# A two-layer decoder trunk on one core: both attention heads of a step together, the imaginary S5 drive from a row-swapped copy of u, and the next step's small loads spread over the step

## The chip, the cores and the metric

The kernel runs on one core of one Trainium2 chip. The metric is the device time of one execution in microseconds. All arithmetic is float32, with the large products in a split form of it. PE is the matrix engine, DVE the vector engine, ACT the scalar engine, POOL the general one, and SP the queue from which most DMAs are issued.

## What is computed

Two layers over x (512 positions x 2048 channels). Each layer scales and shifts x by values from a conditioning vector, projects it to twelve groups of 512 channels, runs four branches on them, and projects their gated outputs back, with a residual and a layer norm.

```python
h = x * (1.0 + scale[:, None]) + shift[:, None]
proj = h @ w_in[l]
y_a = a_b * causal_dwconv(a_c * a_x, conv_a[l]) * jax.nn.silu(a_g)
y_b = dilated_attention(q, k, v, rel_bias).reshape(Bsz, S, BR) * jax.nn.silu(b_g)
y_c = rglru_branch(c_x, conv_c[l], conv_c_b[l], ...) * jax.nn.silu(c_g)
y_d = s5_branch(d_u, ...) * jax.nn.silu(d_g)
y = jnp.concatenate([y_a, y_b, y_c, y_d], axis=-1) @ w_out[l]
x = layer_norm(ALPHA * x + (1.0 + gate[:, None]) * y, ln_g[l], ln_b[l])
```

Attention has 8 heads of 64 channels; its three dilation patterns are merged into one causal softmax with an additive bias per head. The S5 branch drives a complex diagonal state of 64 per group of 16 channels: a real and an imaginary drive (`bu_re`, `bu_im`), a scan, and an output product.

## The kernel before

After a prologue (conditioning sums, bias tables, the transposed and scaled x in `op_hi` and `op_lo`), each layer runs a **branch loop** of four steps (`CT`), and then the output projection (L917 to L945). A step handles 128 channels of every one of the twelve groups, so two attention heads (h = 0, 1) and four S5 tiles (q = 0 to 3).

**PE** walks a step in 24 halves (`HALF`), n = 0 to 23: two for each of the twelve units in `UNITS`. A half is 24 matmuls of 128x512: sixteen with the high part of the weights (L886, L887) and eight with the low part (L893). After half n PE does the small parts that `put(n, ...)` placed there (L856 to L874): `s5_drive` (two matmuls of 32 rows, real into bank 2 and imaginary into bank 3, L785), `s5_output` (L791, L792), `lru_gates` (L801), `scores` (64 rows, L811), `p_turn` (transposes of the probabilities, L820), `weigh` (probabilities times v, 64 columns, L828), `v_turn` and `ada_sum` (L846). These small float32 matmuls stand in the trace as two passes each. Score banks are 5 and 6. Before the change, tiles t of one head alternate between them, and the second head waits until the first has left the banks.

**The weights**: SP loads a half's slice into `raw` (L387), ACT writes `w_hi` (L553) and the negated slice `w_lo` (L556), and POOL issues a DMA that adds `raw` to `w_lo` (L505). PE waits for that DMA before L893.

**SP** issues in program order. Between the slices stand the pieces of `w_ada` for the conditioning of the next part (`ada_load`, L379), which wait until DVE has consumed an earlier piece: two per place in layer 0, one in layer 1. After the last half come the ten small loads of the next step (`step_loads`, L353): S5 and LRU parameters and two bias tiles.

**DVE** runs one list per step (L1001 to L1166), every dependent operation waiting for the one before: parameters of the step, the convolution, per S5 tile `s5_tile` (six operations in, the scan with its carries, six out), the LRU, `score_max` (scores plus bias with a running maximum, L1087; it frees the score bank), `normalise` (L1095), and the gates. `ada(2, 1)` consumes two pieces in layer 0 and one in layer 1. **ACT** does the exponentials of a head (`exps`, L591), copies of transposed probabilities (`p_copy`, L599) and evictions of units, between the weight splits.

```python
for q, (at_drive, at_output) in enumerate(((5, 9), (7, 12), (10, 16), (13, 19))):
...
for h, at in ((0, 10), (1, 17)):
    for t in range(ST):
        put(at + t // 2, scores, h, t)
```

## Time and profile before

| | |
|---|---|
| median of 3 runs | 1981.57 us (1981.14 to 1985.36) |
| profiled execution, its own time | 1983.35 us |
| its span, first to last instruction | 1981.6 us |
| PE busy (matmul) | 1793.6 us, 91% |
| DVE / ACT / POOL busy | 1251.7 / 767.1 / 232.9 us |
| mean granted clock of PE | 0.947 of full speed |
| share of PE in the chain that ended last | 65% (DVE 25%, DMA 4%) |

Times in the trace are microseconds from the start of the span. A row of a timeline gives start, busy time, engine, line, operation, output and input, shape, count, and in brackets the idle time before it and what ended that. Busy times of matmuls overlap: the start of the next row tells when PE was done with issuing the group.

### The profile page before, as it was taken

How to read it: one execution, taken by the hardware profiler on the slowest of the kernel's cores; microseconds unless marked ns; L12 is line 12 of the kernel's file. 1: busy time of each engine (PE TensorE's matmuls, PEld its weight loads, DVE VectorE, ACT ScalarE, POOL GpSimd, SP SyncE). 2: the span in 40 equal slices, each digit the busy share in tenths (PEclk: the TensorE clock that was granted, in tenths of full speed). 3: DMA queues.
4: the chain of work that ended last, by engine and by line, in shares of the span. 5: the costliest groups of instructions: out<-in, count | busy, mean ns of one | idle time of the engine just before them, and what ended most of it. 6: DMA issues, size and time to landing. Idle time of an engine off the chain costs nothing.

```text
span 1981.6 us, 22817 instructions
## 1 busy us (share of the span) xinstructions
PE 1793.6 (91%) x7335; PEld 1323.1 (67%) x7335; DVE 1251.7 (63%) x2361; ACT 767.1 (39%) x1014; POOL 232.9 (12%) x281
## 2 busy tenths in 40 slices
PE   2359999999999999989996999999999999979993
PEld 1347677667667766658885767766876776748882
DVE  5976863883586488456663585486478368543656
ACT  2235344344444443431116544444444454441110
POOL 2331111111111111100004111111111111100000
PEclk9569999999899999999997999999999999989997
DMA  7999679678777986737656867866976886727322
GB/s 274 375 308 236 168 197 216 175 190 208 179 192 194 219 209 161 201 113 258 191 170 177 198 162 181 204 165 168 210 181 154 198 193 167 171 64 255 132 91 85
DMA packets 322945, 376.07 MB, mean 190 GB/s; under 512 B 27064, under 2 KB 224032, under 8 KB 319784
## 3 DMA queue, kind: packets, MB, share of 16 engines
q1 hardware_dynamic: 294632, 272.36, 42.8%
q0 software_dynamic: 28224, 102.77, 28.2%
q8 instruction: 26, 0.43, 0.1%
q14 instruction: 63, 0.52, 0.1%
HBM read 261.81 MB, written 10.51 MB: 137 GB/s over the span
## 4 chain that ended last, share of the span: by engine, by line
PE 65%; DVE 25%; DMA 4%; issue 4%; ACT 1%; SPq 1%; DVEq 0%; POOL 0%; ACTq 0%; POOLq 0%
PE bank L886 12%; PE bank L893 12%; PE bank L887 12%; DVE work L1185 8%; PE bank L931 6%; PE bank L930 6%; PE bank L942 6%; DVE work L1193 3%; DVE ada_acc L1193 3%; PE bank L828 2%; PE bank L811 2%; PE bank L785 2%; PE bank L905 2%; DVE work L1061 2%; DVE work L1062 2%
## 5 line engine op out<-in xcount | busy, mean ns | idle before, releaser
L886 PE MATMUL bank<-op_hi,w_hi 128*128 128x512 f32 x1536 | 625.2, 407 | 0.0
L887 PE MATMUL bank<-op_lo,w_hi 128*128 128x512 f32 x1536 | 607.9, 396 | 0.0
L553 ACT ACTIVATE w_hi<-raw 128x1024 fp32r<-128x1024 f32 x196 | 207.7, 1060 | 525.2 <-PE bank L887 470.9
L893 PE MATMUL bank<-op_hi,w_lo 128*128 128x512 f32 x1536 | 382.6, 391 | 12.0 <-DMA w_lo<-raw 12.0
L886 PEld LDWEIGHTS bank<-op_hi,w_hi 128*128 128x128 f32 x1536 | 293.8, 191 | 113.7 <-issue 54.5
L893 PEld LDWEIGHTS bank<-op_hi,w_lo 128*128 128x128 f32 x1536 | 288.8, 189 | 75.3 <-DMA w_lo<-raw 15.5
L887 PEld LDWEIGHTS bank<-op_lo,w_hi 128*128 128x128 f32 x1536 | 293.8, 191 | 60.8 <-issue 1.9
L505 POOL DMA_DIRECT2D w_lo<-raw x196 | 170.5, 870 | 1198.1 <-ACT w_lo L556 1175.5
L1193 DVE SCALAR_TENSOR_TENSOR ada_acc<-ada_in,cond,ada_acc 128x512 f32<-128x512 f32 (+1 forms) x234 | 181.5, 776 | 132.9 <-DMA ada_in<-in_w_ada 117.5
L556 ACT ACTIVATE w_lo<-raw 128x1024 fp32r<-128x1024 f32 x196 | 207.0, 1056 | 127.4 <-PE bank L893 127.3
L930 PE MATMUL bank<-w_hi,op_hi 128*128 128x512 f32 x512 | 200.0, 391 | 0.0
L931 PE MATMUL bank<-w_hi,op_lo 128*128 128x512 f32 x512 | 199.2, 389 | 0.0
L702 ACT ACTIVATE w_hi<-raw 128x1024 fp32r<-128x1024 f32 x60 | 63.7, 1062 | 248.2 <-PE bank L931 242.4
L1185 DVE TENSOR_TENSOR w_lo<-raw,w_hi 128x1024 fp32r<-128x1024 f32 x60 | 73.5, 1225 | 118.7 <-PE bank L942 115.5
L1185 DVE TENSOR_TENSOR work<-bank,rot 128x512 f32<-128x512 f32 x128 | 88.4, 690 | 65.1 <-PE bank L785 61.5
L942 PE MATMUL bank<-w_lo,op_hi 128*128 128x512 f32 x512 | 126.4, 389 | 0.0
L1185 DVE TENSOR_TENSOR work<-work 128x512 f32<-128x512 f32 (+2 forms) x170 | 112.6, 662 | 5.8
L930 PEld LDWEIGHTS bank<-w_hi,op_hi 128*128 128x128 f32 x512 | 96.1, 188 | 20.4 <-issue 0.5
L931 PEld LDWEIGHTS bank<-w_hi,op_lo 128*128 128x128 f32 x512 | 96.1, 188 | 20.4 <-issue 0.5
L942 PEld LDWEIGHTS bank<-w_lo,op_hi 128*128 128x128 f32 x512 | 96.1, 188 | 19.9
L1185 DVE TENSOR_TENSOR work<-work,rot 128x512 f32<-128x512 f32 x128 | 88.4, 690 | 3.3
L514 POOL TENSOR_TENSOR op_lo<-work,op_hi 128x512 fp32r<-128x512 f32 x32 | 51.5, 1618 | 308.2 <-ACT work L570 307.6
(203 smaller groups left out, 1625.8 us busy)
## 6 DMA issues: line engine op xcount, KB each, us to landing
w_lo<-raw POOLq DMA_DIRECT2D x196, 512.0 KB, 4.7
raw<-in_w_in SPq DMA_DIRECT2D x192, 512.0 KB, 4.0
ada_in<-in_w_ada SPq DMA_DIRECT2D x256, 256.0 KB, 4.4
raw<-in_w_out SPq DMA_DIRECT2D x64, 512.0 KB, 4.1
raw<-in_w_ada SPq DMA_DIRECT2D x27, 512.0 KB, 7.0
ada_in<-in_w_ada SPq DMA_DIRECT2D x18, 512.0 KB, 7.1
rot<-in_w_ada SPq DMA_DIRECT2D x10, 512.0 KB, 6.6
bias_t<-in_w_ada SPq DMA_DIRECT2D x9, 512.0 KB, 7.1
```

The source lines that it names most:

```text
L505: pool.dma_start(w_lo[:, n % NHL, :], raw[:, n % NRAW, :], accum_op=ALU.add)\
L553: act.activation(w_hi[:, n % NHL, :], raw[:, n % NRAW, :], ACT.Copy).then_inc(s.hi_done.sem, 1)
L556: act.activation(w_lo[:, n % NHL, :], raw[:, n % NRAW, :], ACT.Copy, scale=-1.0)\
L702: act.activation(w_hi[:, n % NHL, :], raw[:, n % NRAW, :], ACT.Copy).then_inc(s.hi_done.sem, 1)
L886: pe.matmul(o, w_hi[:, n % NHL, w], op_hi[:, k, :], start=k == 0, stop=False)
L887: mm = pe.matmul(o, w_hi[:, n % NHL, w], op_lo[:, k, :], start=False, stop=False)
L893: mm = pe.matmul(o, w_lo[:, n % NHL, w], op_hi[:, k, :], start=False, stop=k == KT - 1)
L930: pe.matmul(o, op_hi[:, k, x_], w_hi[:, n % NHL, w_], start=k == 0, stop=False)
L931: mm = pe.matmul(o, op_lo[:, k, x_], w_hi[:, n % NHL, w_], start=False, stop=False)
L942: mm = pe.matmul(o, op_hi[:, k, x_], w_lo[:, n % NHL, w_], start=False, stop=k == KT - 1)
L1185: return dve.tensor_tensor(o, a, b, op)
L1193: return dve.scalar_tensor_tensor(o, a, sc, b, op0, op1)
```

## The change

Six things change in the branch loop:

- The scores of both heads are computed together: tile t of head 0 goes to bank 5 and of head 1 to bank 6, each in two column pieces that alternate between the heads. They stand behind halves 9, 10, 12 and 13.
- `p_turn` and `weigh` take both heads in three groups of key blocks (`TURNS`), behind halves 16, 18, 20 and 18, 20, 22. The matmuls of `weigh` alternate between the heads, whose outputs are columns 0 to 63 and 64 to 127.
- Exponentials are head by head after halves 15 and 16 on ACT, both waiting for the one maximum signal. Probabilities of head 1 lie in other buffers (`prob_of`).
- The imaginary drive reads `u_swap`, a copy of u with its two 64-row halves exchanged, so that its rows are 64 away from those of the real drive. ACT makes the copy in two operations of 64 rows, and DVE writes the imaginary coefficients in two operations more per step.
- `s5_tile` is split into `s5_in`, `s5_scan` and `s5_out`, and DVE's list is reordered around `score_max`.
- The loads of the next step are split: LRU behind slice 12, bias behind slice 18, S5 at the end.

```diff
+u_swap = work[:, 17, :]
-p_t = work[:, 14:16, :]
+p_t = [(work[:, 14, :], work[:, 15, :]), (q_t, k_t)]
+prob_of = [[prob[:, at:at + P * (t + 1)] for t, at in enumerate(P_AT)],
+           [ada_acc[:, 2, 0:P], prob[:, 1280:1536], ada_acc[:, 2, P:S], v_t]]
+
+TURNS = ((0,), (1, 3), (2,))
+TURN_AT = {0: 0, 1: 0, 3: 3 * P, 2: 0}
...
-        def step_loads(step):
+        def s5_loads(step):
...
+        def lru_loads(step):
+
+            if step:
+                sp.wait_ge(s.full[6].sem, s.full[6].at(1, step - 1))
...
+        def bias_loads(step):
+
+            if step:
+                sp.wait_ge(s.to_act.sem, s.to_act.at(2, step - 1))
...
+                if step < CT - 1:
+                    if n == 12:
+                        lru_loads(step + 1)
+                    if n == 18:
+                        bias_loads(step + 1)
...
             if step < CT - 1:
-                step_loads(step + 1)
+                s5_loads(step + 1)
...
+            def p_copy(g):
+                n = sum(P * (ST - kb) for kb in TURNS[g])
+                if g != 1:
+                    act.wait_ge(s.pv_done.sem, s.pv_done.at(g, ct))
+                for h in range(2):
+                    act.wait_ge(s.full[5 + h].sem, s.full[5 + h].at(1 + ST + g + 1, ct))
+                    act.activation(p_t[h][g % 2][:, 0:n], bank[5 + h][:, 0:n], ACT.Copy).then_inc(s.p_copy.sem, 1)
...
-                    copy("d_u", u_d)
+                    ps, free = unit("d_u")
+                    act.wait_ge(s.gate_used[1].sem, s.gate_used[1].at(0, ct))
+                    act.activation(u_d, ps, ACT.Copy)
+                    for h in range(2):
+                        swapped = act.activation(u_swap[64 * h:64 * h + 64, :], ps[64 - 64 * h:128 - 64 * h, :], ACT.Copy)
+                    swapped.then_inc(free.sem, 1)
...
                 if n == 13:
-                    exps(0)
                     gate("c_g", 0, 0)
...
+                if n in (15, 16):
+                    exps(n - 15)
                 if n == 15:
+                    act.wait_ge(s.full[3].sem, s.full[3].at(SQ, ct))
                     gate("d_g", 1, 0)
-                if n == 16:
-                    p_copy(0, 0)
-                    p_copy(0, 1)
+                if n in (18, 20, 22):
+                    p_copy((n - 18) // 2)
...
-                    fill(2 + i, pe.matmul(bank[2 + i][:, :], s5_w[32 * q:32 * q + 32, i, :],
-                                          u_d[32 * q:32 * q + 32, :], start=True, stop=True))
+                for i, u in enumerate((u_d, u_swap)):
+                    row = 32 * ((q + 2 * i) % SQ)
+                    fill(2 + i, pe.matmul(bank[2 + i][:, :], s5_w[row:row + 32, i, :], u[row:row + 32, :],
+                                          start=True, stop=True))
...
+                n = P * (t + 1)
+                for h in range(2):
+                    is_free(5 + h, 1 + t)
+                for w in (slice(0, n // 2), slice(n // 2, n)):
+                    for h in range(2):
+                        heads = slice(64 * h, 64 * h + 64)
+                        mm = pe.matmul(bank[5 + h][:, w], q_t[heads, P * t:P * (t + 1)], k_t[heads, w],
+                                       start=True, stop=True)
...
+                for kb in TURNS[g]:
+                    n = P * (ST - kb)
+                    for w in (slice(0, n // 2), slice(n // 2, n)) if kb % 2 else (slice(0, n),):
+                        for h in range(2):
+                            mm = pe.matmul(bank[7][64 * h:64 * h + 64, P * kb + w.start:P * kb + w.stop],
...
+            for t, at in enumerate((9, 10, 12, 13)):
+                put(at, scores, t)
             put(11, v_turn)
-            for h, at in ((0, 14), (1, 21)):
...
+            for g, (at_turn, at_weigh) in enumerate(((16, 18), (18, 20), (20, 22))):
+                put(at_weigh, weigh, g)
+                put(at_turn, p_turn, g)
...
-        s5_tile(1, 2, 1)
-        score_max(0, (0, 1))
-        ada(2, 1)
-        score_max(0, (2, 3))
-        ada(2, 1)
+        score_max(0)
+        s5_in(1)
+        s5_scan(1)
+        ada(2, 1)
+        score_max(1)
+        s5_out(1)
+        ada(2, 1)
+        score_max(2)
+        s5_in(2)
+        ada(2, 1)
+        score_max(3)
+        s5_scan(2)
+        ada(2, 1)
+        s5_out(2)
         normalise(0)
-        s5_tile(2, 2, 1)
+        ada(2, 1)
+        normalise(1)
         own(silu2(0, "c_g", gx[:, 0, :]), s.own)
...
-        s5_tile(3, 2, 1)
-        score_max(1, (0, 1))
-        ada(2, 1)
-        score_max(1, (2, 3))
+        s5_in(3)
+        s5_scan(3)
+        ada(2, 1)
+        s5_out(3)
```

**PE behind half 10** (`raw` slice 10, `work` holds u, q, k, their copies and the probabilities). Before, the drive of tile 2 and the first two score tiles of head 0:

```order
L785 MATMUL bank<-work,s_w 128x512 [waits free2_0]
L785 MATMUL bank<-work,s_w 128x512 [waits free3_0]
L811 MATMUL bank<-work 128x128 [waits free5_0,free1_0,free0_0]
L763 REGISTER_ALU
L811 MATMUL bank<-work 128x256 [waits free6_0]
```

Now, at the same place:

```order
L807 MATMUL bank<-work,s_w 128x512 [waits free3_0,free2_0]
L807 MATMUL bank<-work,s_w 128x512
L783 REGISTER_ALU [waits free5_0]
L835 MATMUL bank<-work 128x128 [waits free6_0]
L835 MATMUL bank<-work 128x128 x3
```

The two drives now wait for both banks at once, and one score tile (t = 1) of both heads stands in four pieces of 128 columns where two tiles of one head stood.

**PE, first `weigh` and the transposes behind it.** Before, behind half 15:

```order
L828 MATMUL bank<-work 64x512 [waits free7_0,p_copy_0]
L825 REGISTER_ALU
L828 MATMUL bank<-work 64x384 [waits p_copy_0]
L820 MATMUL bank<-ident,work 128x128 [waits p_copy_0,p_norm_0]
L820 MATMUL bank<-ident,work 128x128
```

Now, behind half 18:

```order
L861 MATMUL bank<-work 64x512 [waits free7_0,p_copy_0]
L861 MATMUL bank<-work 64x512
L849 MATMUL bank<-ident,work 128x128 [waits p_copy_0]
L849 MATMUL bank<-ident,work 128x128 x3
L849 MATMUL bank<-ident,work 128x128 [waits p_copy_0]
```

Key block 0 of both heads stands side by side, three halves later, and blocks 1 and 3 are turned behind it.

**SP at the end of a step.** Before:

```order
L380 DMA ada_in<-in_w_ada 128x512 [waits ada_used_0] x2
L363 DMA work<-in_s_b_re 128x4x16 [waits to_act_0,c_done_0]
L363 DMA work<-in_s_b_im 128x4x16
L367 DMA work<-in_s_c_re 128x64
L367 DMA work<-in_s_c_im 128x64
L372 DMA lru_w<-in_lru_wa 64x64 x2
L372 DMA lru_w<-in_lru_wx 64x64 x2
L375 DMA bias_t<-bias_tile_scratch 128x512 x2
L387 DMA raw<-in_w_in 128x8x128 [waits raw_used_0] x2
```

Now, behind slice 12 of the step, and at its end:

```order
L399 DMA raw<-in_w_in 128x8x128 [waits raw_used_0]
L379 DMA lru_w<-in_lru_wa 64x64 [waits full6_0]
L379 DMA lru_w<-in_lru_wa 64x64
L379 DMA lru_w<-in_lru_wx 64x64 x2
L399 DMA raw<-in_w_in 128x8x128 [waits raw_used_0]
```

```order
L365 DMA work<-in_s_b_re 128x4x16 [waits c_done_0]
L365 DMA work<-in_s_b_im 128x4x16
L369 DMA work<-in_s_c_re 128x64
L369 DMA work<-in_s_c_im 128x64
L399 DMA raw<-in_w_in 128x8x128 [waits raw_used_0] x2
```

Four of the ten loads remain between the last slice of a step and the first of the next.

## Rows read from the trace of the kernel before

**Rows 1.** Busy time of two of the eight steps of the branch loop, core 0, microseconds

```profile
309.00:485.50 176.50, 171.02 (x690) 123.05 (x690) 116.53 (x246) 75.02 (x100) 20.85 (x24) 0.97 0.79 194
...
1412.60:1578.20 165.60, 164.61 (x681) 119.69 (x681) 104.40 (x229) 76.72 (x101) 20.83 (x25) 1.00 0.77 182
```

**Rows 2.** Timeline of PE, layer 1, third step: start, busy, line

```profile
1438.43 1.98 PE L893 MATMUL bank<-op_hi,w_lo 128*128 128x512 f32 x8
...
1443.88 1.97 PE L893 MATMUL bank<-op_hi,w_lo 128*128 128x512 f32 x8
...
1445.78 1.98 PE L785 MATMUL bank<-work,s_w 32*128 32x512 f32 x4
...
1451.45 1.97 PE L893 MATMUL bank<-op_hi,w_lo 128*128 128x512 f32 x8
...
1458.65 1.97 PE L893 MATMUL bank<-op_hi,w_lo 128*128 128x512 f32 x8
```

**Rows 3.** The same timeline: `weigh` (L828), then `scores` (L811) of one head

```profile
1519.75 1.72 PE L828 MATMUL bank<-work 128*64 128x512 f32 x4
...
1521.40 0.55 PE L820 MATMUL bank<-ident,work 128*128 128x128 f32 x3
...
1529.19 0.86 PE L828 MATMUL bank<-work 128*64 128x256 f32 x4
...
1535.65 0.92 PE L811 MATMUL bank<-work 64*128 64x128 f32 x4
...
1542.17 1.77 PE L811 MATMUL bank<-work 64*128 64x384 f32 x4
```

**Rows 4.** The same timeline: the eight passes of `ada_sum`

```profile
1577.12 1.05 PE L846 MATMUL bank<-ones,ada_acc 128*128 128x1 f32 x8
```

**Rows 5.** Waits of PE over the whole span: total, times, longest

```profile
PE bank L811 <- DVE soft L1087: 12.9, 8, 3.9
```

**Rows 6.** Timeline of PE, layer 0, after halves 10 and 12 of two steps

```profile
385.23 1.97 PE L893 MATMUL bank<-op_hi,w_lo 128*128 128x512 f32 x8
...
402.88 1.98 PE L893 MATMUL bank<-op_hi,w_lo 128*128 128x512 f32 x8
...
731.46 1.98 PE L893 MATMUL bank<-op_hi,w_lo 128*128 128x512 f32 x8
...
754.85 1.98 PE L893 MATMUL bank<-op_hi,w_lo 128*128 128x512 f32 x8
```

**Rows 7.** Timelines of PE and of SP, layer 0, around step boundaries

```profile
344.96 2.55 PE L893 MATMUL bank<-op_hi,w_lo 128*128 128x512 f32 x8 [3.16 <-DMA w_lo<-raw]
...
347.44 3.78 PE L785 MATMUL bank<-work,s_w 32*128 32x512 f32 x4
...
466.73 2.16 SPq L372 DMA_DIRECT2D lru_w<-in_lru_wx  x2
...
502.06 1.13 SPq L380 DMA_DIRECT2D ada_in<-in_w_ada  x2
```

**Rows 8.** Timeline of DVE, layer 1, third step

```profile
1492.96 0.69 DVE L1087 CUSTOM_DVE_ANT_0 work<-bank,bias_t 128x512 f32<-128x512 f32 x1
...
1496.45 1.66 DVE L1189 TENSOR_SCALAR work<-work,soft 128x128 f32<-128x128 f32 x4
...
1498.14 1.42 DVE L1185 TENSOR_TENSOR work<-bank,rot 128x512 f32<-128x512 f32 x2
...
1502.49 0.42 DVE L1061 TENSOR_TENSOR_SCAN work<-s_k,work 128x128 f32<-128x128 f32 x1
...
1509.30 0.75 DVE L1193 SCALAR_TENSOR_TENSOR ada_acc<-ada_in,cond,ada_acc 128x512 f32<-128x512 f32 x1
...
1509.97 1.41 DVE L1185 TENSOR_TENSOR work<-work,rot 128x512 f32<-128x512 f32 x2
```

**Rows 9.** End of a step on DVE, and the wait of PE behind a layer's loop

```profile
1582.28 0.43 DVE L1189 TENSOR_SCALAR y_t<-work 128x512 f32 x1 [0.16 <-DVE work L1193]
...
846.79 13.80 PE L905 MATMUL bank<-y_t,work 128*128 128x512 f32 x26 [9.36 <-DMA work<-in_s_w_glu]
```

More of the change, by code:

```diff
@@ L61 @@
 ADA_PLACES = 16
-OWN_STEPS = (168, 167)
+OWN_STEPS = (170, 169)
 ROWS = {}
@@ L814, in p_turn @@
-                    def p_turn(h, kb):
-                        b = 5 + kb % 2
-                        pe.wait_ge(s.p_norm.sem, s.p_norm.at(h + 1, ct))
-                        if kb >= 2:
-                            pe.wait_ge(s.p_copy.sem, s.p_copy.at(ST * h + kb - 1, ct))
-                        for t in range(kb, ST):
-                            mm = pe.transpose(bank[b][:, P * (t - kb):P * (t - kb + 1)],
-                                              prob[:, P_AT[t] + P * kb:P_AT[t] + P * (kb + 1)], ident[:, :])
-                        fill(b, mm)
@@ L824, in weigh @@
-                    def weigh(h, kb):
-                        pe.wait_ge(s.p_copy.sem, s.p_copy.at(4 * h + kb + 1, ct))
-                        if h == 0 and kb == 0:
-                            is_free(7, 1)
-                        pe.matmul(bank[7][64 * h:64 * h + 64, P * kb:S], v_s[:, kb, 64 * h:64 * h + 64],
-                                  p_t[:, kb % 2, 0:P * (ST - kb)], start=kb == 0, stop=kb == ST - 1)\
-                            .then_inc(s.pv_done.sem, 1)
+                        n = P * (t + 1)
@@ new lines, in p_turn @@
+                    def p_turn(g):
+                        for h in range(2):
+                            if g == 0:
+                                pe.wait_ge(s.p_norm.sem, s.p_norm.at(h + 1, ct))
+                            else:
+                                pe.wait_ge(s.p_copy.sem, s.p_copy.at(2 * (g - 1) + h + 1, ct))
+                            for kb in TURNS[g]:
+                                for t in range(kb, ST):
+                                    at = TURN_AT[kb] + P * (t - kb)
+                                    mm = pe.transpose(bank[5 + h][:, at:at + P], prob_of[h][t][:, P * kb:P * (kb + 1)],
+                                                      ident[:, :])
+                            fill(5 + h, mm)
@@ new lines, in weigh @@
+                    def weigh(g):
+                        pe.wait_ge(s.p_copy.sem, s.p_copy.at(2 * g + 2, ct))
+                        if g == 0:
+                            is_free(7, 1)
+                        for kb in TURNS[g]:
+                            n = P * (ST - kb)
+                            for w in (slice(0, n // 2), slice(n // 2, n)) if kb % 2 else (slice(0, n),):
+                                for h in range(2):
+                                    mm = pe.matmul(bank[7][64 * h:64 * h + 64, P * kb + w.start:P * kb + w.stop],
+                                                   v_s[:, kb, 64 * h:64 * h + 64],
+                                                   p_t[h][g % 2][:, TURN_AT[kb] + w.start:TURN_AT[kb] + w.stop],
+                                                   start=kb == 0, stop=kb == 2)
+                                    if w.stop == n:
+                                        mm.then_inc(s.pv_done.sem, 1)
@@ L1077, in s5_tile, with score_max @@
                     own(tt(x_im, x_im, t_, ADD), s.x_rot)
-                def score_max(h, ts_):
-                    for t in ts_:
-                        b, use = 5 + t % 2, 1 + 4 * h + t // 2
-                        w = P * (t + 1)
-                        dve.wait_ge(s.full[b].sem, s.full[b].at(use + 1, ct))
-                        dve.wait_ge(s.mix_in.sem, s.mix_in.at(96, ct))
+                def score_max(t):
+                    for h in range(2):
+                        b, i, w = 5 + h, ST * h + t, P * (t + 1)
+                        dve.wait_ge(s.full[b].sem, s.full[b].at(1 + t + 1, ct))
+                        if t == 0 and h == 0:
+                            dve.wait_ge(s.mix_in.sem, s.mix_in.at(96, ct))
+                        if t == ST - 1 and h == 1:
+                            dve.wait_ge(s.full[7].sem, s.full[7].at(1, ct))
                         line(dve.memset(spare[:, :], 0.0), s.own)
-                        own(dve.tensor_tensor_reduce(prob[:, P_AT[t]:P_AT[t] + w], bank[b][:, 0:w],
-                                                      bias_t[:, h, S - w:S], 1.0, -3e38, ADD, ALU.max,
-                                                      soft[:, 0, t:t + 1]), s.free[b])
-                    if ts_[-1] == 3:
+                        own(dve.tensor_tensor_reduce(prob_of[h][t], bank[b][:, 0:w], bias_t[:, h, S - w:S], 1.0, -3e38,
+                                                      ADD, ALU.max, soft[:, 0, i:i + 1]), s.free[b])
+                    if t == ST - 1:
                         own(ts(soft[:, 1, :], soft[:, 0, :], -1.0, MUL), s.to_act)
@@ L1094, in normalise @@
                     dve.wait_ge(s.from_act.sem, s.from_act.at(3 + h, ct))
-                    own(dve.reciprocal(soft[:, 3, :], soft[:, 2, :]), s.own)
+                    w = slice(ST * h, ST * h + ST)
+                    own(dve.reciprocal(soft[:, 3, w], soft[:, 2, w]), s.own)
                     for t in range(ST):
-                        pt = prob[:, P_AT[t]:P_AT[t] + P * (t + 1)]
-                        own(ts(pt, pt, soft[:, 3, t:t + 1], MUL), s.own if t < 3 else s.p_norm)
+                        i = ST * h + t
+                        own(ts(prob_of[h][t], prob_of[h][t], soft[:, 3, i:i + 1], MUL), s.p_norm if t == ST - 1 else s.own)
                 def silu2(i, use_name, dst):
@@ L1103, in silu2 @@
                     return stt(dst, gt[:, i, :], 1.0, gx[:, i, :], ADD, MUL)
-                s5_tile(0, 2, 1)
+                s5_in(0)
+                s5_scan(0)
+                ada(2, 1)
+                s5_out(0)
                 ada(2, 1)
```

96 lines of the change are left out of this document (34 added, 62 removed).

## The prediction, made before the changed kernel ran

> **What bounds the kernel now.** I first read busy times step by step [rows 1]. A step of layer 1 takes 165.6 us and PE is busy for 164.6 of them, with the other engines at 21 to 104. So PE's own list sets the time there: a microsecond off that list is a microsecond gained in each of 4 steps, as long as nobody makes PE wait instead. A step of layer 0 takes up to 176.5 us with 171.0 busy; its surplus is waits, and passes at a lower clock (0.97 against 1.00).
>
> Then PE's timeline, to price the small parts. A plain half lasts 5.45 us; with a drive behind it 7.57, so a drive costs 2.13; with `lru_gates` behind it (also four passes of 512 columns, but on all rows and columns) 7.20, so 1.76 [rows 2]. The drive's group is busy for 1.98 us of which the last 0.07 overlaps what follows: 1.91, or 0.48 a pass, and 0.22 more for coming and going. The tiles that this change touches pay such a 0.22 each time they stand alone behind a half. `scores` of one head take 0.92 and 1.77 us less 0.07 each, so 2.55; `weigh` of one head takes 1.65 and 0.86 less 0.07, so 2.44 [rows 3]. All of these fit a pass of 0.05 us and 0.83 ns per column, down to a floor: eight passes of one column take 1.05 us less 0.07, so 0.12 each, which is the time of bringing in their weights [rows 4].
>
> Third, PE's waits: 12.9 us in 8 waits of `scores` for a bank that `score_max` frees [rows 5], one per step behind half 11. Two cost more than their idle time. From the low product of half 10 to that of half 12 an ordinary layer 0 step takes 17.65 us, one with the longest wait of 3.9 us takes 23.39 [rows 6]: 5.7 more for at most 2.6 more idle, since PE ran at the lower clock behind it. I read the same, 3.2 us on top, in the first step.
>
> Last, the step boundaries of layer 0. PE waits 3.16 us for `w_lo` at half 5, and the following group and drive take 2.55 and 3.78 us where 1.98 is usual [rows 7]. The cause stands on SP: at 502.06 it gets past an `ada_load` that had waited for DVE's first pieces of the step, and the slices behind it are late.
>
> **The change, part by part**, against the profiled execution (1983.35 us by its own time; the median of the runs is 1.8 lower).
>
> *Drives.* No row shows two small tiles of different rows side by side, so whether they overlap is the main unknown. If they don't, a drive stays at 1.91. If they do, and passes start in program order with two passes of one instruction one after the other, then A1, A2 beside B1, B2 take three slots instead of four: 1.43. I take three slots, since the operands are placed 64 rows apart, in different banks, and nothing in the rows forbids it. Gain 0.48 x 4 = 1.9 a step. Full overlap (two slots) would double it.
>
> The Trainium skill (TensorE: Matmul & The Clock Gate, Part 3: Packing small matmuls) says that matmuls on different rows of the array run together, four of 32 rows at 3.07 times the speed; no run shown here tests it. If both passes of both drives fell together as it describes for single matmuls, the sum below would be some 30 us lower for drives and pairs together.
>
> *Scores.* Per tile t there are now eight passes of 64, 128, 192 and 256 columns, in five slots, but with eight weight loads at the floor of 0.12: 0.96, 0.96, 1.05 and 1.32, together 4.3 for 5.1 before. In series they would take 6.0. They now all stand next to an output or a drive, so three lonely visits (behind 11, 17, 18) save 0.22 each. Gain 0.8 + 0.66 = 1.5 a step.
>
> *Weigh.* Blocks 0 and 2 take three slots (1.43 and 0.79), blocks 1 and 3 in halves 1.05 and the floor 0.96: 4.2 for 4.9. In series: 5.6. Visits: three alone before, three now. Gain 0.7. The 20 transposes stay.
>
> Together 4.1 a step, 33 us over 8 steps.
>
> *The old bank waits go*: the second head no longer shares them, and DVE takes a tile's maximum at least half a PE half before the banks are wanted. 12.9 and two times 3.2: 19 us.
>
> *New waits.* I walked DVE's new list between its anchors, with 4.35 us for `s5_in` or `s5_out`, 6.8 for the scan, 0.67 for a piece, 0.8 for the widest maximum (0.69 and its small companions), 1.9 for `normalise` [rows 8]. From the last scores in the banks to both heads normalised: 1.6 + 0.2 + 6.8 + 0.7 + 4.35 + 1.9 + 0.7 + 1.9 = 18.1. PE has three halves, an output and four transposes: 16.3 + 2.1 + 0.4 = 18.9 before it wants head 1. So 0.8 to spare in layer 1, and with one piece more at two places 0.6 short in layer 0. From the first scores to the second output: 1.2 + 4.35 + 6.8 + 0.7 + 1.4 + 4.35 = 18.8 against 16.3 + 2.6 + 0.6 = 19.5; again spare in layer 1, 0.7 short in layer 0 with its later start. The third drive wants banks that `s5_in` frees 0.4 to 0.7 us earlier. I allow 8 us in all, for four steps at 1.3 and some latencies.
>
> *ACT* gains two copies of half the rows (some 1.2 us) behind half 3, where it idles; the exponentials hold up its weight split by about 0.3 us. *DVE*'s two extra operations (0.4) stand ahead of a wait. Both cost nothing while PE is the bound; if that cover goes, 1.6 us a step.
>
> *SP.* LRU loads now stand ahead of slice 13. Two of them hold SP for 2.16 us [rows 7], so the four some 3.3; a slice is issued about 9 us before its split. I cost it at nothing and keep up to 3 us a step for the range. At the boundary SP issues six loads less.
>
> *Boundary.* Before, DVE ends a step 4.5 us after PE (1582.71 against 1577.12 + 1.05) [rows 4, 9], since `weigh` is the last thing PE does. Now `weigh` ends one half earlier and only the last projection and the `ada_sum` are left: about 2.3 us after. The first pieces of the next step are then consumed 2 us earlier, which shortens the two stalls of layer 0 (4 us each with some 5.5 at the low clock). Between 3 us (shorter only) and 19 (gone): I take 9, since half of it hangs on whether the clock still falls. The same 2 us come off the 9.4 us that PE waits for `w_glu` behind each loop [rows 9], as that load follows DVE's last operation: 4 us.
>
> Sum: -33 - 19 + 8 - 9 - 4 = -57: 1926, and 1.8 less against the median: **1925 us**.
>
> **Rivals.**
>
> - *Column pairs don't overlap* (only `weigh`): 5.6 in place of 4.2 a step, +11: 1936. For it: both heads use all rows; against it: they write different partitions.
>
> The Trainium skill (same page, Part 3) states that weight loads overlap with running matmuls only when the row group differs, which is not so in `weigh`; no run shown here tests that either. It would give this rival's time.
>
> - *Nothing overlaps*, so the pairing doesn't do what it is laid out for. Drives gain 0, scores lose 0.9 and win 0.66, weigh loses 0.7: +1 a step, +8. PE is later everywhere, so new waits shrink to 3. 8 - 19 + 3 - 5 - 4 = -17: 1965. For it: no row shows an overlap of two small tiles, and all of them pay to come and go.
> - *Layer 0 hangs on its transfers*: SP's moved loads and two pieces per place keep the four steps as long as now but for the bank waits. 16 + 9 us come back: 1950. For it: a DMA share of 0.79 [rows 1] that grows with speed.
> - *Slower.* DVE's chain decides: all of its new places have under 1 us to spare. If `normalise` of head 1 or the third `s5_in` came 4 us late, PE would idle 3.9 and run 3.2 us slow as it did in the longest wait: 7 us. Everything else gains 8.1 a step, so one such wait per step leaves 9 us of gain, and two cost 14.2: +49, 2031. It decides from 8.1 us of loss per step. For it: the chain; against: the lists leave 0.8, and a slower PE gives DVE room.
> - *No change*, should small gains and waits cancel.
>
> **How the numbers follow.** Forecast 0.60 (its own range 1905 to 1942), column pairs 0.12, no overlap 0.11, transfers 0.08, slower 0.06, no change 0.03. A measurement of this kernel tells 0.2% (4 us) from nothing. Faster by more: 0.60 + 0.12 + 0.11 + 0.08 less 0.03 for cases that fall short = 0.88; within 0.2%: 0.04; slower: 0.08. The range goes from full overlap (two slots for a pair and no boundary stall: 1903) to the case without overlap (1966).
>
> **What would show it.** In the profile after: a drive's group busy for about 1.5 us in place of 1.98, with starts of its second and third pass together; `scores` of the widest tile at 1.3; layer 1 steps of 161 us. `scores` should no longer wait for a bank, and `p_turn` for `p_norm` by up to 1 us in layer 0. DVE's last operation should end 2.3 us after PE's step. Wrong would be: drive groups of 1.9 us (no overlap), waits of PE above 2 us at `p_turn`, `s5_output` or the drives (DVE bound), or `w_lo` waits inside the steps of layer 0 (transfers).

## The result and the profile after

| | before | after |
|---|---|---|
| median of the runs compared | 1983.09 us (1981.14 to 1985.36) | 1881.33 us (1880.44 to 1882.28) |
| profiled execution, its own time | 1983.35 us | 1880.47 us |
| mean granted clock of PE | 0.947 | 0.956 |

After over before is 0.9488, 95% interval 0.9469 to 0.9507. The change saves 102 us where 57 were forecast, and 1881 lies below the range, which began at 1903. The direction was right, the size was not.

Busy time of a step of each layer in the profile after, as in [rows 1] (first layer 0, then layer 1):

```profile
300.62:459.70 159.08, 157.38 (x714) 118.84 (x713) 116.43 (x246) 76.72 (x100) 20.82 (x24) 1.00 0.87 216
...
1486.80:1643.00 156.20, 156.17 (x704) 117.86 (x703) 104.80 (x229) 77.93 (x102) 20.84 (x24) 1.00 0.79 187
```

A step of layer 1 now takes 156.2 us in place of 165.6, with PE busy throughout: PE is still the bound there. The step is 9.4 us shorter: 8.4 of PE's list, where 4.1 were forecast, and 1.0 of the old wait for a score bank. Layer 0 gains 17.4 us in the step shown and its clock is back at 1.00. The tiles that the change touched, layer 1, last step of PE's timeline (drive; then `scores` of tiles 0 to 3 for both heads; then `weigh` in its three groups):

```profile
1575.82 1.13 PE L807 MATMUL bank<-work,s_w 32*128 32x512 f32 x4
...
1547.88 0.66 PE L835 MATMUL bank<-work 64*128 64x64 f32 x8
...
1555.21 0.71 PE L835 MATMUL bank<-work 64*128 64x128 f32 x8
...
1569.30 0.92 PE L835 MATMUL bank<-work 64*128 64x192 f32 x8
...
1576.88 1.14 PE L835 MATMUL bank<-work 64*128 64x256 f32 x8
...
1608.25 1.08 PE L861 MATMUL bank<-work 128*64 128x512 f32 x4
...
1623.33 1.10 PE L861 MATMUL bank<-work 128*64 128x192 f32 x16
...
1635.86 0.65 PE L861 MATMUL bank<-work 128*64 128x256 f32 x4
```

The drive's four passes are busy for 1.13 us and the next group starts 1.06 after them, where [rows 2] had 1.98 and 1.91. `scores` of both heads take 0.66 + 0.71 + 0.92 + 1.14 less 4 x 0.07, so 3.15 for 5.1 of [rows 3]; `weigh` takes 2.83 less 0.21, so 2.6 for 4.9. A pair costs 0.54 to 0.62 of what its two tiles cost in series, the column pairs of `weigh` as well as the row pairs. The weight loads show how. Before, the drive at 1445.78 of [rows 2]:

```profile
1445.78 0.29 PEld L785 LDWEIGHTS bank<-work,s_w 32*128 32x128 f32 x2 [0.35 <-issue]
1446.32 0.18 PEld L785 LDWEIGHTS bank<-work,s_w 32*128 32x128 f32 x1 [0.24 <-issue]
1446.74 0.18 PEld L785 LDWEIGHTS bank<-work,s_w 32*128 32x128 f32 x1 [0.24 <-issue]
```

and after, a drive and a `weigh` of 512 columns:

```profile
1575.82 0.30 PEld L807 LDWEIGHTS bank<-work,s_w 32*128 32x128 f32 x4 [0.35 <-issue]
...
1608.25 0.20 PEld L861 LDWEIGHTS bank<-work 128*64 128x64 f32 x4 [0.35 <-issue]
```

Before, the third and fourth loads come one pass apart (1446.32, 1446.74). After, all four are done within 0.3 us. I read this as both tiles having their first weights in the array and their second ones waiting, so that the two passes of one run beside the two of the other.

PE's waits in the loops and for `w_glu`, after (the wait of `scores` for a bank, [rows 5], is gone):

```profile
PE bank L934 <- DMA work<-in_s_w_glu: 16.2, 2, 8.5
...
PE bank L922 <- DMA w_lo<-raw: 4.4, 3, 2.5
PE bank L849 <- DVE work L1238: 4.2, 4, 1.1
...
PE bank L813 <- DVE work L1234: 2.6, 4, 0.6
```

The last two are the new ones, in layer 0 only, 6.8 us in all. The three waits for `w_lo` lie in the first steps of the layers; the two stalls of 3.2 and 3.6 us at half 5 are gone. The steps of layer 0 by the starts of `ada_sum`, before:

```profile
307.10 1.95 PE L846 MATMUL bank<-ones,ada_acc 128*128 128x1 f32 x16
...
483.51 1.95 PE L846 MATMUL bank<-ones,ada_acc 128*128 128x1 f32 x16
...
661.27 1.95 PE L846 MATMUL bank<-ones,ada_acc 128*128 128x1 f32 x16
...
835.48 1.95 PE L846 MATMUL bank<-ones,ada_acc 128*128 128x1 f32 x16
```

and after:

```profile
296.37 1.84 PE L882 MATMUL bank<-ones,ada_acc 128*128 128x1 f32 x16
...
455.49 1.84 PE L882 MATMUL bank<-ones,ada_acc 128*128 128x1 f32 x16
...
614.60 1.84 PE L882 MATMUL bank<-ones,ada_acc 128*128 128x1 f32 x16
...
773.69 1.84 PE L882 MATMUL bank<-ones,ada_acc 128*128 128x1 f32 x16
```

So 176.4, 177.8 and 174.2 us became 159.1 three times. Before, the first two steps had a stall at the boundary and a short wait for the score bank, the third no stall but the longest bank wait (3.9). That pairing was in the trace of before, and it matters below.

### The profile page after: what moved, and what is told of

Same layout as the page of the kernel before. It is cut to its first block, busy times and chain, and to the rows that moved or that the text cites. A ratio compares the mean times of both kernels' runs of the same rounds, so it can differ in the third digit from the quotient of the medians.

```text
span 1878.6 us, 23043 instructions
## 1 busy us (share of the span) xinstructions
PE 1707.7 (91%) x7527; PEld 1299.5 (69%) x7527; DVE 1253.3 (67%) x2369; ACT 778.3 (41%) x1014; POOL 232.6 (12%) x281
## 4 chain that ended last, share of the span: by engine, by line
PE 69%; DVE 21%; issue 4%; DMA 2%; SPq 1%; ACT 1%; POOL 0%; DVEq 0%; ACTq 0%; POOLq 0%
PE bank L915 14%; PE bank L922 14%; PE bank L916 14%; DVE work L1234 6%; PE bank L959 6%; PE bank L960 6%; PE bank L971 6%; DVE ada_acc L1242 3%; DVE work L1242 3%; PE bank L934 2%; DVE y_t L1242 1%; DVE work L1096 1%; DVE work L1095 1%; PE bank L807 1%; PE bank L861 1%
## 5 line engine op out<-in xcount | busy, mean ns | idle before, releaser
L915 PE MATMUL bank<-op_hi,w_hi 128*128 128x512 f32 x1536 | 615.7, 401 | 0.0
L916 PE MATMUL bank<-op_lo,w_hi 128*128 128x512 f32 x1536 | 601.2, 391 | 0.0
L915 PEld LDWEIGHTS bank<-op_hi,w_hi 128*128 128x128 f32 x1536 | 289.5, 189 | 88.2 <-issue 22.2
L916 PEld LDWEIGHTS bank<-op_lo,w_hi 128*128 128x128 f32 x1536 | 289.7, 189 | 59.8 <-issue 1.9
```

What stands on the lines that cost most here:

```text
L915: pe.matmul(o, w_hi[:, n % NHL, w], op_hi[:, k, :], start=k == 0, stop=False)
L916: mm = pe.matmul(o, w_hi[:, n % NHL, w], op_lo[:, k, :], start=False, stop=False)
```

## Experiments

Ratios are to the kernel before on the same chip, with 95% intervals; the changed kernel stands at 0.9488.

| run | median us | ratio |
|---|---|---|
| e1 same rows | 1905.59 | 0.9616 (0.9598 to 0.9635) |
| e2 swap alone | 1977.15 | 0.9969 (0.9951 to 0.9988) |
| e3 loads at end | 1882.24 | 0.9500 (0.9482 to 0.9517) |
| e4 late weigh | 1901.96 | 0.9598 (0.9570 to 0.9626) |
| e5 whole tiles | 1882.81 | 0.9485 (0.9460 to 0.9510) |
| e6 head by head | 1881.09 | 0.9479 (0.9456 to 0.9502) |
| e7 pieces later | 1876.60 | 0.9463 (0.9444 to 0.9482) |
| e8 w_glu early | 1868.83 | 0.9429 (0.9409 to 0.9449) |
| e9 all three | 1862.19 | 0.9392 (0.9374 to 0.9411) |
| e10 long tail | 1886.40 | 0.9510 (0.9487 to 0.9533) |
| e11 tail and loads | 1886.68 | 0.9513 (0.9490 to 0.9536) |
| e12 longer tail | 1906.30 | 0.9609 (0.9589 to 0.9630) |
| e13 pieces after slice | 2031.47 | 1.0250 (1.0220 to 1.0281) |
| e14 one place late | 1975.98 | 0.9971 (0.9954 to 0.9988) |
| e15 best | 1858.61 | 0.9372 (0.9354 to 0.9391) |

### The drives: e1 and e2

In the changed kernel:

```diff
-                        for i, u in enumerate((u_d, u_swap)):
-                            row = 32 * ((q + 2 * i) % SQ)
-                            fill(2 + i, pe.matmul(bank[2 + i][:, :], s5_w[row:row + 32, i, :], u[row:row + 32, :],
-                                                  start=True, stop=True))
+                        for i in range(2):
+                            fill(2 + i, pe.matmul(bank[2 + i][:, :], s5_w[32 * q:32 * q + 32, i, :],
+                                                  u_d[32 * q:32 * q + 32, :], start=True, stop=True))
...
```

> The changed kernel, but the imaginary drive reads the same 32 rows of u as the real one (the swapped copy is still made and read by nobody). Theory (two slots): in the changed kernel's trace a drive's four passes start in pairs and take 1.06 us instead of 1.91, because matmuls on different rows run side by side in both of their passes. Then the group goes back to 1.91, +0.85 x 32 = +27 us, less up to 5 us of layer 0's waits that the slower PE covers: 1903 to 1909. Rival (placing): the passes come together because both bank waits now stand ahead of both matmuls, whatever their rows; then nothing changes, 1881. The prediction's three slots would give +15, 1896.

1905.6 us, +24: the rows are what matters, and the second output no longer waits, as expected of a slower PE (27.2 less 2.6). The group's row reads as before the change:

```profile
1557.09 1.98 PE L806 MATMUL bank<-work,s_w 32*128 32x512 f32 x4
```

The same part by itself, in the kernel before:

```diff
...
-                        for i in range(2):
+                        for i, u in enumerate((u_d, u_swap)):
                             is_free(2 + i, q)
...
+                            row = 32 * ((q + 2 * i) % SQ)
...
```

> The kernel before, with nothing but the row-swapped drive (its copy of u, its two extra operations on DVE; the wait for the second bank still stands between the two matmuls). Theory (two slots): a drive's group takes 1.06 instead of 1.91, -27 us of 1983: 1956; a few us less gain if the waits for score banks grow by what PE gains ahead of them (half 10's drive stands just before them). Rival (placing): no gain, 1983 or 1 to 2 more for ACT's copies.

1977.2 us: a gain of 6, not 27. The drive did get faster, also with the wait between its matmuls, but the score bank took it back:

```profile
1666.35 1.13 PE L793 MATMUL bank<-work,s_w 32*128 32x512 f32 x4
```

```profile
PE bank L819 <- DVE soft L1094: 34.2, 8, 6.0
```

12.9 us of waiting became 34.2, and in every step of layer 1 the group behind the wait now runs at the lower clock in part or whole (2.35 to 3.35 us busy where 1.83 was usual):

```profile
1480.97 3.35 PE L819 MATMUL bank<-work 64*128 64x384 f32 x4 [2.59 <-DVE soft L1094]
```

The 27 us of drives less the 21 of new waiting come to the 6 that were measured; the waits for `w_lo`, 5 us shorter, and the lower clock are not priced in this. A faster PE only reaches sooner what DVE frees at its own time. 24 us at one end and 6 at the other: the row pairing is worth its price only together with the new order of scores and DVE's list. The two parts are not additive.

### How the passes of a pair overlap: e5 and e6

```diff
-                        for w in (slice(0, n // 2), slice(n // 2, n)):
-                            for h in range(2):
+                        for h in range(2):
+                            heads = slice(64 * h, 64 * h + 64)
+                            fill(5 + h, pe.matmul(bank[5 + h][:, 0:n], q_t[heads, P * t:P * (t + 1)], k_t[heads, 0:n],
...
```

> The changed kernel with every score tile and every block of weigh as one matmul per head, no column pieces: head 0, then head 1. Theory (own order): a set of rows, or of columns, takes its passes in its own order and doesn't wait for the other set, so two whole neighbours also run in two slots, and half of the weight loads go: per step some 0.6 us of scores and 0.1 of weigh less, 1875 to 1878 against 1881.3. Rival (program order): passes start in the order of the program, A1 A2 B1 B2 in three slots; the pieces are what made the scores overlap; then scores go from 3.1 to 3.8 and weigh's blocks 1 and 3 from 1.0 to 1.6 a step: +10, 1891.

> The changed kernel with the same column pieces, but both pieces of head 0 before those of head 1 (scores, and weigh's blocks 1 and 3). Theory (own order, looks far ahead): head 1's passes start although four of head 0 stand before them; no change, 1881. Rival (neighbours only): of A, A', B, B' only A' and B run side by side, three slots for two: scores +1.2 and weigh +0.5 a step, +14: 1895.

In e6 the two loops, over pieces and heads, change places. Neither order lengthens anything. The whole tiles of 128, 256, 384 and 512 columns, head 0 then head 1:

```profile
1552.57 0.49 PE L834 MATMUL bank<-work 64*128 64x128 f32 x4
...
1559.72 0.70 PE L834 MATMUL bank<-work 64*128 64x256 f32 x4
...
1573.79 0.92 PE L834 MATMUL bank<-work 64*128 64x384 f32 x4
...
1581.38 1.13 PE L834 MATMUL bank<-work 64*128 64x512 f32 x4
```

and, in e6, the eight passes of the widest tile, the four of head 0 first:

```profile
1578.55 1.14 PE L835 MATMUL bank<-work 64*128 64x256 f32 x8
```

Both take half of the slots that the passes would take in series: two for the four of a whole tile pair, four for the eight in pieces. So program order doesn't hold back a tile on other rows: head 1 starts although up to four passes of head 0 stand ahead of it. That is the prediction's error in one line. (The Trainium skill, TensorE: Matmul & The Clock Gate, Part 3, says that matmuls start and end strictly in program order. Taken pass by pass that would give three slots in e5, and matmul by matmul six in e6, where four of 256 columns are measured. The measurement decides.) The column pieces buy nothing for the overlap. They cost a load only at the narrowest tile (0.66 against 0.49), 0.2 us a step, and the time didn't move: I had expected 0.7 a step less. The floor of 0.12 us a pass of [rows 4] was read from passes in series; the eight passes of 64 columns on two sets of rows take 0.59 us, so 0.07 each.

### Why layer 0's boundary stalls went: e3, e4, e10, e11, e12

e3 puts the LRU and bias loads back behind `s5_loads` at the step's end.

> The changed kernel with all ten small loads of the next step again at the end of a step. Theory (DVE's tail): layer 0's boundary waits went because DVE now ends a step 2.4 us after PE instead of 4.5 and so takes the next step's first pieces of w_ada 2.9 us earlier, which lets SP issue the following slices 2.5 us earlier; the place of the loads does next to nothing: 1881 to 1884, no wait for w_lo at halves 4 and 5. Rival (loads): SP was late because it issued ten loads (5.4 us) between two slices at the boundary; then the waits of 3 us come back at three boundaries, with the low clock behind them, +19: 1900.

1882.2: the place of the small loads is worth nothing, and no stall came back. e4 sets `TURNS` one half later: places (17, 19), (19, 21), (21, 23), and ACT's copies with them.

> The changed kernel with the three groups of p_turn and weigh one half later each, so that the last weigh stands behind half 23 as before the change and DVE's tail is longer again (4.5 us after PE). Theory (DVE's tail): waits for w_lo at halves 4 and 5 come back at the three boundaries of layer 0, +10 to +19, the wait for w_glu grows by 2 us per layer (+4), and layer 0's waits of p_turn for head 1 (4.2 in all) go: 1891 to 1900. Rival (loads): the boundary stays free, only w_glu +4 and p_turn -4: 1881.

1902.0, but only part of it for the reason given. The stalls came back, 3.0 us at one boundary, 0.5 to 1.3 at all three, and the wait for `w_glu` grew by 3.2. But most of the +21 is another wait, at the fourth output of layer 0:

```profile
PE bank L813 <- DVE work L1234: 14.8, 12, 2.8
...
PE bank L922 <- DMA w_lo<-raw: 9.2, 7, 3.0
```

With less PE work ahead of half 19, PE meets DVE's chain there. So in layer 0 of the changed kernel DVE is just in time at that output. To have the tail by itself, e10 lengthens it:

```diff
...
                 dve.wait_ge(s.from_act.sem, s.from_act.at(5, ct))
+                for _ in range(2):
+                    own(tt(s5_s[2], y, y, MUL), s.own)
+                own(dve.tensor_copy(s5_s[2], y), s.own)
                 own(stt(y, gel, 1.0, y, ADD, MUL), s.own)
```

> The changed kernel with three useless operations on DVE ahead of its last two of every step, 2.2 us, so that it ends a step about 4.6 us after PE as before the change, and nothing else moved. Theory (DVE's tail alone): the waits for w_lo at halves 4 and 5 of layer 0 come back (before: 4.1 and 4.3 us at two boundaries, with the low clock behind), +8 to +15, and the waits for w_glu grow by 2 x 2.2 = 4.4: 1893 to 1900. Rival (the tail is no cause): only w_glu, 1886.

1886.4. Mostly the rival: the waits at half 5 did not come back, those at half 4 did, with 0.7 to 0.9 us. e11 has e10's edit and e3's.

> The long tail on DVE and, besides, all ten small loads at the end of the step on SP: the two together as before the change. Theory (DVE's tail alone): as with the long tail alone, within 2 us. Rival (both needed): the long tail alone costs only w_glu's 4.4 and a little of w_lo, and this one 8 to 15 us more.

1886.7: the loads don't matter with the long tail either. So my theory stood in doubt: DVE's tail had nearly its old length (the three operations took 1.9 us; DVE's last operation ends 4.1 us after PE in layer 0, before the change 4.3) and the stall of half 5 stayed away. The timelines of SP and ACT show what is left. The slice of half 5 stands on SP behind two `ada_load`s that wait for DVE's first piece, and its split waits for it. SP after, at the boundary of 455.49:

```profile
470.97 1.59 SPq L392 DMA_DIRECT2D ada_in<-in_w_ada  x2
472.60 0.74 SPq L399 DMA_DIRECT2D raw<-in_w_in  x1
```

and the split of that slice on ACT, after and before (before, the slice was issued at 503.23, right behind the row at 502.06 of [rows 7]):

```profile
478.85 1.06 ACT L575 ACTIVATE w_hi<-raw 128x1024 fp32r<-128x1024 f32 x1 [3.93 <-DMA raw<-in_w_in]
```

```profile
510.71 1.06 ACT L553 ACTIVATE w_hi<-raw 128x1024 fp32r<-128x1024 f32 x1 [7.67 <-DMA raw<-in_w_in]
```

Six boundaries of layer 0 read in this way, in us from the start of `ada_sum`:

| kernel, boundary | slice issued | split starts | waits at halves 4 and 5 |
|---|---|---|---|
| after, second | 17.1 | 23.4 | 0, 0 |
| e10, first | 18.4 | 24.8 | 0.9, 0 |
| before, third | 18.6 | 25.1 | 0, 0 |
| e4, first | 19.2 | 27.7 | 0.5, 3.0 |
| before, first | 19.6 | 27.8 | 1.0, 3.2 |
| before, second | 19.7 | 27.2 | 0.7, 3.6 |

(At before's third boundary PE itself was 1.6 us later, so the slice had that much more time.) At the six other boundaries of the changed kernel, e10 and e4 the slice was issued at 17.4 to 18.7, was split 5.6 to 6.6 us later, and half 5 did not wait. So up to 18.7 a slice is split 5.6 to 6.6 us after its issue, from 19.2 on 7.5 to 8.5 after it. That is a cliff: 0.6 us later in issue, some 2 us later again in landing, and DVE's tail moves the kernel along it. It doesn't do so alone. Between the last operation of a step and the first of the next DVE has a gap, which was 5.4 and 5.6 us at before's two stalled boundaries and 4.0 and 4.1 at the first two of e10. With it e10, in spite of nearly the old tail, issues the slice 1.2 and 1.3 us earlier than before the change. In e4, too, the stalled boundary is the one with the longest gap (4.8 against 4.2 and 4.3). e12 goes further, with six useless operations, which took 3.8 us:

> The changed kernel with six useless operations at the end of DVE's step instead of three, 4.4 us in place of 2.2. Theory (a cliff): with 2.2 us the slice of half 5 was issued 18.4 us after the start of ada_sum and split 6.4 us later, in time; before the change it was issued at 19.6 to 19.7 and split 7.5 us later, and with weigh later at 19.2 and 8.5, both times with a wait of 3 to 3.6 us at half 5. Here it is issued at about 20.5, so all three boundaries of layer 0 get the wait of 3 us or more besides the 0.9 at half 4, and some 5 us of low clock: +24 to +30, and w_glu's 2 x 4.4 = 8.8: 1910 to 1920. Rival (in proportion): the next 2.2 us cost what the first did, 5 us: 1891.

1906.3, +25: nearer to the cliff (1910 to 1920) than to proportion (1891). The stall is back at the first and third boundary:

```profile
333.15 3.69 PE L922 MATMUL bank<-op_hi,w_lo 128*128 128x512 f32 x8 [2.58 <-DMA w_lo<-raw]
...
659.65 2.77 PE L922 MATMUL bank<-op_hi,w_lo 128*128 128x512 f32 x8 [3.13 <-DMA w_lo<-raw]
```

The slices were issued at 19.3, 19.4 and 19.3 there, and the second (19.4) was still split 6.1 us later, the others 9.0 and 8.6. So the edge lies between 18.7 and 19.4 and isn't sharp. What delays a slice beyond it is not settled. POOL issues the DMA of `w_lo` for half 4 at 19.7 to 19.8 at all of these boundaries but before's third (21.4), and the traces give the time from issue to landing of both transfers (512 KB each, medians over a whole run 4.0 to 4.2 us for a slice and 4.7 to 5.0 for `w_lo`):

| boundaries | slice issued | slice landed after | `w_lo` landed after |
|---|---|---|---|
| after, all three | 17.1 to 17.5 | 5.5 to 6.1 | 7.0 to 7.3 |
| before, third | 18.6 | 6.3 | 7.6 |
| e10, all; e4, second and third | 18.4 to 18.7 | 5.9 to 6.5 | 8.8 to 9.4 |
| before, first two; e4, first; e12, first and third | 19.2 to 19.7 | 7.4 to 8.9 | 8.7 to 9.3 |
| e12, second | 19.4 | 6.0 | 9.6 |

With the two issues 2.2 to 2.8 us apart the two landings add up to 12.6 to 13.9 us, with 1.0 to 1.4 apart to 14.8 to 15.9, with 0.1 to 0.6 apart to 15.6 to 17.9, and at e12's second boundary `w_lo` alone bore the delay. The waits at half 4 are the late landing of this `w_lo`. That the two transfers slow each other fits these rows, but no run moved the issue of `w_lo`, so it is not shown.

### What the stalls were worth before: e13 and e14

In the kernel before, on SP, so that the slice of half 5 stands ahead of the waiting loads:

```diff
+                            late = 1 if l == 0 and place >= 2 else 0
-                            if max(3 * place // 2 + 1, 1 + place, 2 - step) == n:
+                            if min(max(3 * place // 2 + 1, 1 + place, 2 - step) + late, HALF - 1) == n:
```

> The kernel before, with layer 0's ada loads from the third place on issued one slice later, so that the slice of half 5 stands ahead of the two loads that wait for DVE's first piece, and nothing else changed. Theory (that order makes the boundary stalls): no wait for w_lo at halves 4 and 5 of layer 0; but PE then comes earlier to the score bank that DVE frees, as in the fourth step, which has no boundary stall, waits 3.9 us for the bank and lasts 174.2 us where the two before it last 176.4 and 177.8: so -6, 1977 against 1983. Rival (contention alone): w_lo is late because of the transfers' number, wherever they stand; no change, 1983. Rival (independent sums): the stalls and their low clock go whole, -19: 1964.

2031.5: no wait for `w_lo` was left behind the first step of layer 0, as the theory has it, but DVE starved, its waits for pieces growing from 117.5 to 222.3 us, and PE waited for DVE at the score bank (30.9 us), the drives (10.5) and the transposes (9.1):

```profile
DVE ada_acc L1194 <- DMA ada_in<-in_w_ada: 222.3, 54, 17.1
```

A miss by 54 us: I had looked at PE's side of the move only. e14 moves one place alone (`place == 2`).

> The kernel before, with only the third place of layer 0 (two ada loads) issued one slice later, so that the slice of half 5 no longer stands behind the two loads that wait for DVE's first piece; the other places stay, since with all of them later DVE starved for pieces (222 us of waits). Theory (that order makes the boundary stalls): no wait for w_lo at halves 4 and 5 in layer 0; the steps after the two stalled boundaries fall from 176.4 and 177.8 to the 174.2 of the one without, as PE then waits longer for the score bank: 1977 against 1983. Rival (what counts is DVE's supply): pieces of the third place come late, DVE's chain and so the score bank too: 1990 or more. Rival (independent sums): 1964.

1976.0 (forecast 1977): no stall at any boundary, three even steps of 172.2, 172.6 and 172.2 us, and longer waits for the score bank in exchange:

```profile
310.57 1.95 PE L847 MATMUL bank<-ones,ada_acc 128*128 128x1 f32 x16
...
482.73 1.95 PE L847 MATMUL bank<-ones,ada_acc 128*128 128x1 f32 x16
```

```profile
PE bank L812 <- DVE soft L1088: 16.9, 7, 3.9
```

So the boundary stalls alone were worth 8 us by the medians (2 to 9 by the interval) in the kernel before, since the next wait was ready to take them. With the bank waits gone too, as in the changed kernel, that next wait is not there.

### Going on: e7, e8, e9, e15

e7 moves the `ada` pieces that stand ahead of `score_max(1)` and between the two `normalise` to behind `s5_out(1)` and `normalise(1)`.

> The changed kernel with two ada pieces of DVE moved behind what PE waits for: the one ahead of the first score_max of tile 1 goes behind s5_out(1), the one between the two normalise behind the second. Theory: layer 0's waits (0.65 at the second output and 1.05 at the transposes of head 1, per step, 6.8 us in all) go, layer 1 stays: 1874.5. Rival: DVE only moves the wait to the fourth output, which came just in time (with weigh later it waited 2.8 us in each step of layer 0): then 0 to 2 us are left of it, 1880.

1876.6, between the two: both old waits went, and 0.8 to 1.0 us appeared at the fourth output. e8 gives `w_glu` the buffers of v and the probabilities:

```diff
-        w_glu = work[:, 5:9, :]
+        w_glu = work[:, 10:14, :]
...
-                    if n == NRAW - 1:
-
-                        sp.wait_ge(s.step_end.sem, s.step_end.at(0, CT))
+                    if n == 1:
+                        sp.wait_ge(s.pv_done.sem, s.pv_done.at(0, CT))
```

> The changed kernel with w_glu in the buffers of v and the probabilities (free once the last weigh is done) instead of S5's, and its load issued behind the output slices 0 and 1 instead of behind DVE's last operation. Theory: PE's waits of 7.7 and 8.5 us behind the loops shrink to what DVE's last operation sets (it ends 2.4 us after PE's last matmul, less its share that overlaps), so about 2 to 3 us each: -11 us, and up to 4 more from the clock behind a shorter wait: 1866 to 1870. Rival: the 1 MB load now stands ahead of the third output slice and makes the first halves of the output projection late by as much: 1881.

1868.8 as expected. The waits of PE shrink to 2.9 and 2.6 us, the second of them now for DVE's last output:

```profile
779.99 10.55 PE L933 MATMUL bank<-y_t,work 128*128 128x512 f32 x20 [2.90 <-DMA work<-in_s_w_glu]
...
1641.17 15.38 PE L933 MATMUL bank<-y_t,work 128*128 128x512 f32 x32 [2.55 <-DVE y_t L1237]
```

> The changed kernel with whole tiles, later ada pieces and the early w_glu together. If each does what its theory says and none gives back: -5 - 7 - 11, about 1858. Rival (DVE bound in layer 0): with PE faster by 0.6 a step and its waits gone DVE's chain decides in layer 0, and 2 to 5 us are given back: 1862.

> The changed kernel with whole tiles, the early w_glu, the two ada pieces later and a third one, the one between scan and output of tile 3, moved behind s5_out(3), since the fourth output still waited 0.85 us per step of layer 0 with the first two moved. Theory: these waits go, 4 x 0.85 = 3.4 less than 1862.2: 1859. Rival (DVE's chain is full in layer 0): another place waits by as much, 1862.

1862.2 for e9 (the rival's number: the fourth output waits 0.85 in each step of layer 0) and 1858.6 for e15, where PE no longer waits for DVE inside the branch loops; the waits for `w_lo` in the first step of each layer (5.3 us) stay. It is 22.7 us below the changed kernel and 6.3% below the one before (ratio 0.9372).

## Why the prediction was wrong

Point by point, against the trace after:

| term | forecast | shown |
|---|---|---|
| drives | 15 | 27 (0.85 x 32) |
| scores | 12 | 21 (5.1 + 0.66 - 3.15 = 2.6 a step) |
| weigh | 6 | 18 (4.9 - 2.6 = 2.3 a step) |
| score bank waits, idle | 13 | 12.9 |
| boundary waits | 9 | 8.4 idle |
| low clock | 6, behind the bank waits | about 17 in steps two to four of layer 0, behind both |
| new waits | -8 | -6.8 |
| `w_glu` | 4 | 2.9 (19.1 - 16.2) |
| sum | 57 | 100 of 102.9 |

- **The step that failed** is in the first part: "passes start in program order with two passes of one instruction one after the other", so "three slots". It is two, for rows and for columns (e1, e5, e6). The terms drives, scores and `weigh` were mis-sized by it alike, 33 us where the rows show 66 to 67, which is 34 of the missing 45 us. Layer 1 checks it free of the rest: 9.4 us a step, of which 8.4 are list and 1.0 the bank wait.
- **The boundary** was the other: "Between 3 us (shorter only) and 19 (gone): I take 9". It was gone, which is 10 us more. The reason given, DVE's shorter tail (I forecast 2.3 us after PE; in layer 0 it ends 2.2 after, at 459.56, where it had ended 4.3 after), is most of what moved the slice, by 2.1 and 2.6 us at the two stalled boundaries. The gap on DVE, shorter by 0.8 and 1.2 us, moved it too, and the prediction had nothing on that. In proportion, as I reckoned, both would have left part of the stall: it is a cliff, and the change stepped back over it. In e10 a slice 1.3 us later cost 5 us, in e12 one 2.2 us later cost 25, `w_glu`'s share of 3 and 7 included.
- **The low clock** was in the bank term as 6 us and vaguely in the boundary's. The steps two to four of layer 0 hold more. They last 528.4 us. Three steps of layer 1's length without its bank wait, with 0.9 for the longer `ada_sum`, are 496.7; the idle time is 15.1; 16.7 remain, which I put down to the clock. The granted clock of the three steps agrees: 0.97, 0.96 and 0.97 of full speed, so by an estimate 0.10 of some 176 us, 17.6. After, the same sum leaves 0.8, at a granted clock of 1.00.
- **Right** were: PE as the bound in layer 1, no new wait there, the places and sizes of layer 0's new waits (forecast 0.6 to 0.7 and up to 1, found 0.65 and 1.05), the loads on SP at nothing (e3), ACT's copies at nothing in layer 1, where PE is busy for 156.17 of 156.20 us, and the fate of the bank waits.
- **The range** broke by its own text. The low end was named as full overlap and no stall. By the text's own numbers that was 30 and 10 us below 1925, so 1885, not 1903, which holds only 12 of the 30. Even 1885 would have left 1881 just outside, since the low clock was too small in the sum.
- **The rivals**: no pair ran in series, and DVE's chain left layer 0 only 1.7 us of wait a step. But e4 shows how near that rival was, with 2.8 us at one output for a single half of delay.

## What to carry to other kernels

In this kernel two float32 tiles on disjoint rows (64 apart) or disjoint columns of the array, standing next to each other, cost little more than one: 1.06 us for a drive that had cost 1.91, and 2.6 for a step's `weigh` that had cost 4.9. The order of the passes did not matter, and splitting the tiles further brought nothing (e5, e6). Before costing a saving on PE, find the wait that it will run into: the same edit was worth 6 us alone and 24 in company, and stalls that by my estimate cost some 19 us with their clock were worth 8 (2 to 9) while another wait stood behind them. A stall that hangs on a queue's order can have an edge: read the time of issue over all repetitions of the loop, also those without the stall.

## What was not expected of the hardware

- The passes of a pair in half of their slots even with all of one head's four passes ahead of the other's (1.14 us for eight passes of 256 columns).
- A slice issued 18.6 us after the start of `ada_sum` was split 6.5 us later, one issued at 19.2 8.5 us later. The 512 KB of `w_lo`, issued at 19.7, landed after 7.0 to 7.3 us with the slice issued by 17.5, and after 8.7 to 9.6 with it issued at 18.4 or later.
- The gap on DVE between the last operation of a step and the first of the next, in which the profile shows no wait but "issue", isn't constant: 5.4, 5.6 and 4.1 us before the change, 4.4 to 4.7 after, 4.0 to 4.3 in e10, 3.1 to 3.3 in e12. In the kernel before, the boundary with 4.1 is the one without a stall. What sets it stays open.
